# Decoder with a mixture of experts: a set's down weights queued ahead of the next set's gate weights

## What is computed

```python
for l in range(DEPTH):                      # DEPTH = 2
    h = rms_norm(x, norm1_g[l])
    proj = h @ w_in[l]                      # 1024 x 3072, then two kinds of attention
    ...
    x = x + jnp.concatenate([o_da, o_sb], axis=-1) @ w_out[l]
    h2 = rms_norm(x, norm2_g[l])
    x = x + hierarchical_moe(h2, ...)

# hierarchical_moe: best group of 4, then the two best of its 8 experts; combine holds their weights
hg = jnp.einsum('sd,edf->sef', hs, w_gate)  # 32 experts, 1024 x 256 each
hu = jnp.einsum('sd,edf->sef', hs, w_up)    # the same size
act = jax.nn.silu(hg) * hu * combine.astype(hs.dtype)[..., None]
return jnp.einsum('sef,efd->sd', act, w_down)   # 256 x 1024 each
```

## Time and profile before

| | us |
|---|---|
| median of 3 runs | 832.82 |
| lowest and highest | 831.23, 833.08 |
| the profiled execution's own time | 830.57 |
| its span, first to last instruction | 828.8 |
| PE busy in the span | 681.0 (82%) |
| DVE busy | 300.5 (36%) |
| ACT busy | 127.5 (15%) |
| DMA queue of SP, share of 16 engines | 72.3% |

### The profile page before, as it was taken

One profiled execution on the slowest core, in us unless ns is written; L12 is line 12 of the kernel. 1 busy time (PEld: TensorE's weight loads), 2 busy tenths in 40 slices (PEclk: granted clock), 3 DMA queues, 4 the chain that ended last, 5 costly groups with the idle time before them and its releaser, 6 DMA issues.

```text
span 828.8 us, 9937 instructions
## 1 busy us (share of the span) xinstructions
PE 681.0 (82%) x3684; PEld 335.2 (40%) x3685; DVE 300.5 (36%) x654; ACT 127.5 (15%) x318; POOL 9.0 (1%) x19
## 2 busy tenths in 40 slices
PE   7998999968865956878699989998788768658684
PEld 5445455643333312442144455646433224124321
DVE  0336622453423322413325364325243324224223
ACT  3115521200000000000031343211000000000000
POOL 0000000010000000000020000000000000000000
PEclk9999999999988878989899989998999889889997
DMA  8798038539999999975993240753299999999551
GB/s 291 238 400 314 1 123 334 202 47 418 421 422 423 421 422 423 421 294 226 387 344 145 102 152 1 270 243 147 95 418 421 422 422 421 422 422 421 236 202 51
DMA packets 49984, 240.03 MB, mean 290 GB/s; under 512 B 7648, under 2 KB 7936, under 8 KB 25376
## 3 DMA queue, kind: packets, MB, share of 16 engines
q1 hardware_dynamic: 49344, 238.61, 72.3%
q0 software_dynamic: 608, 0.99, 1.0%
HBM read 238.54 MB, written 1.05 MB: 289 GB/s over the span
## 4 chain that ended last, share of the span: by engine, by line
PE 54%; DMA 22%; issue 11%; DVE 5%; PEldq 2%; PEld 2%; ACT 1%; SPq 1%; DVEq 1%; ACTq 1%
PE bank L1020 19%; DMA wbuf<-in_w_down 18%; PE bank L1167 7%; PE bank L1117 7%; PE bank L1145 5%; PE bank L1184 5%; PE bank L1195 3%; DMA wbuf<-in_w_up 3%; PE bank L1077 1%; PEldq L1186 1%; PE bank L1064 1%; DMA wbuf<-in_w_in 1%; SPq L326 1%; PE bank L1097 1%; PE bank L1040 1%
## 5 line engine op out<-in xcount | busy, mean ns | idle before, releaser
L1020 PE MATMUL bank<-wbuf,hTbuf 128*128 128x512 f32 x384 | 170.3, 600 | 2.6 <-DMA wbuf<-in_w_in 2.1
L1184 PE MATMUL bank<-wbuf,qkT 128*32 128x512 f32 x512 | 80.6, 758 | 62.5 <-DMA wbuf<-in_w_down 56.0
L1167 PE MATMUL bank<-wbuf,qkT 128*32 128x512 f32 x1024 | 113.2, 594 | 2.0 <-DVE qkT L756 1.1
L1020 PEld LDWEIGHTS bank<-wbuf,hTbuf 128*128 128x128 f32 x384 | 72.7, 192 | 90.7 <-issue 88.3
L1145 PE MATMUL bank<-qkT,xn 128*128 128x128 f32 x512 | 68.6, 297 | 29.2 <-issue 29.2
L1145 PEld LDWEIGHTS bank<-qkT,xn 128*128 128x128 f32 x512 | 65.5, 211 | 42.2 <-issue 42.1
L783 DVE TENSOR_TENSOR x_sb<-x_sb,bank 128x512 f32<-128x512 f32 x72 | 46.3, 684 | 77.9 <-PE bank L1195 77.9
L1167 PEld LDWEIGHTS bank<-wbuf,qkT 128*32 128x32 f32 x1024 | 32.5, 110 | 79.4 <-issue 76.3
L1184 PEld LDWEIGHTS bank<-wbuf,qkT 128*32 128x32 f32 x512 | 16.3, 128 | 116.4 <-issue 58.5
L1117 PE MATMUL bank<-wbuf,hTbuf 128*128 128x512 f32 x128 | 56.0, 593 | 0.0
L776 DVE COPY qkT<-bank 128x512 f32<-128x512 f32 x16 | 11.1, 692 | 93.6 <-PEq L1186 93.6
(11 more groups left out here) (195 smaller groups left out, 592.8 us busy)
## 6 DMA issues: line engine op xcount, KB each, us to landing
wbuf<-in_w_gate SPq DMA_DIRECT2D x64, 1024.0 KB, 21.5
wbuf<-in_w_up SPq DMA_DIRECT2D x64, 1024.0 KB, 21.9
wbuf<-in_w_down SPq DMA_DIRECT2D x64, 1024.0 KB, 16.1
wbuf<-in_w_in SPq DMA_DIRECT2D x24, 1024.0 KB, 14.2
wbuf<-in_w_out SPq DMA_DIRECT2D x8, 1024.0 KB, 6.2
x_sb<-in_x SPq DMA_DIRECT2D x2, 512.0 KB, 4.5
out<-x_sb SPq DMA_DIRECT2D x1, 1024.0 KB, 4.0
cst<-in_const SPq DMA_DIRECT2D x1, 548.0 KB, 13.8
```

The costliest lines, as they stand in the source:

```text
L1020: last = MM(ps[PROJ_BANK[i][t]][:, :], hT[:, k, t * P:(t + 1) * P], block_rows(i, k), start=(k == 0), stop=(k == KC - 1))
L1167: MM(ps[bank][j * SLOTS:(j + 1) * SLOTS, :].rearrange("p (a f) -> p a f", a=2), src[:, k, j * SLOTS:(j + 1) * SLOTS], halves[:, gate:up + ...
L1184: MM(ps[banks[h]][j * SLOTS:(j + 1) * SLOTS, :], src[:, c, j * SLOTS:(j + 1) * SLOTS], at[j][:, c * D + h * HALF:c * D + (h + 1) * HALF], ...
```

## The change

In `load_further_sets` the wait for `dn_used` and the four down parts behind it are moved ahead of the four gate parts of the next set. Nothing else is changed: the same DMAs, the same slots, the same waits.

```diff
                     sp_.wait_ge(gu_used, l * SETS + g)
                     load_up(l, g, LANES - 1)
+                    sp_.wait_ge(dn_used, l * SETS + g)
+                    for j in range(LANES):
+                        load_down(l, g, j)
                     if g + 1 < SETS:
                         for j in range(LANES):
                             load_gate(l, g + 1, j)
-                    sp_.wait_ge(dn_used, l * SETS + g)
-                    for j in range(LANES):
-                        load_down(l, g, j)
```

## The result

The changed kernel takes 851.73 us as a median of 4 runs (850.85 to 852.89), the kernel before 832.95 of 4 (831.23 to 834.24). The ratio is 1.0228 with a 95% interval of 1.0204 to 1.0252, 18.8 us slower. The forecast was 851. The profiled execution took 850.98 us, with a span of 849.2 against 828.8.

The account below looks back on a forecast made before the run. The prediction took transfers to set the pace up to `gate_up` of set 6, then PE. Delays of 7.9 and 6.8 us plus 3.8 for the clock made 18.5 us, so 851 us as a median, range 845 to 855.

Parts of the forecast that it names:

- The step that no down part's early landing could help: At `gate_up` of set 6, PE follows the last up part; earlier down parts bring nothing beyond 0.2 to 0.4 us.
- The hole: At each layer's first wait in `load_further_sets`, held gate parts leave the queue empty: 7.9 and 6.8 us late.
- the restart: At set 1, the empty queue's first part lands 4.7 us after issue, then each further part after 2.49.
- The later sets: Behind set 1, `dn_used` comes 12.2 or 10 us before the queue's end, so the queue stays full.
- The clock: PE's rest moves ahead of `gate_up` of set 6, which runs at a lower clock: 1.9 us a layer, 3.8 in all.
- The stop of 2.25 us in the gather: Layer 0, before `dn_used` of set 0: PE's stop for issue might shrink by 0 to 2.25 us; taken as 0.
- The sum: Whole kernel: 7.9 + 6.8 + 3.8 = 18.5 us slower, giving a median of 851 us.
- The estimate at 2.93 us a part: At the skill page's 358 GB/s transfer rate, the two layers' shifts would be some 8.4 and 7.7 us.
- a hole in every set: Rival: `dn_used` comes after the queue's end in sets 2 to 6, 74 us more, 925 us; chance 0.04.
- a covered hole: Rival: queue still busy at the first wait, or PE slack at set 6, swallows the delay: 833 us; chance 0.04.
- the waits given back: Rival: PE's eight waits for down parts vanish, up to 56 us back, about 792 us; chance 0.03.
- part of the sum: Rival: the clock stays up and the 2.25 us stop shrinks, 12.4 us slower, 845 us; within the forecast case's 0.89.

Follow-up runs that it names:

- e3: Kernel before with the new order in the sets 2 to 4 alone: 835.18 us, ratio 1.0009 to the kernel before.
- e12: Kernel before, order of transfers kept, but at set 1 SP waits for `dn_used` ahead of the gate parts of set 2: 850.76 us, ratio 1.0203.
- e2: Kernel before with the new order in set 1 alone: 853.27 us, ratio 1.0208 to the kernel before.
- e5: Changed kernel with two of the four gate parts of set 2 ahead of the wait of set 1: 843.97 us, ratio 1.0120 to the kernel before.
- e6: Changed kernel where SP at set 1 also waits until `gate_up` of set 1 is done: 877.81 us, ratio 1.0552 to the kernel before.
- e1: Kernel before with the new order in the sets 2 to 6 alone, set 1 unchanged: 839.66 us, ratio 1.0084 to the kernel before.
- e4: Kernel before with the new order in set 5 alone: 837.07 us, ratio 1.0028 to the kernel before.
- e7: Changed kernel with 46 small unused matmuls in PE's rest ahead of the `gate_up` of set 6: 848.60 us, ratio 1.0186 to the kernel before.
- e10: Kernel before with 5 and 3 unused 512-column matmuls in PE's rests behind `gate_up` of set 6 and set 7: 821.43 us, ratio 0.9860.
- e8: Kernel before with 40 and 22 small unused matmuls in PE's rests behind `gate_up` of set 6 and set 7: 910.68 us, ratio 1.0919.
- e9: Changed kernel with 5 unused 512-column matmuls in PE's rest ahead of `gate_up` of set 6: 848.62 us, ratio 1.0191 to the kernel before.

## Why the prediction was right

**The place of the loss.** The step that no down part's early landing could help, since the queue's last up part of set 6 is what PE runs into, held: PE's waits for down parts went from 56.0 us to none and the kernel got slower. The order as such costs nothing that could be measured (e3, at most 2.8 us), and without any change of order the wait costs the same within the intervals (e12).

**The hole.** Predicted 7.9 and 6.8 us, measured 9.0 and 8.2 from set 0 to set 6. Here a term was too small, by 1.1 and 1.4 us: the restart. I took 4.7 us and then 2.49 a part, which puts the landing of the fourth down part some 10.8 us behind its issue; it took 12.4. The trace shows one step out of line in each layer, between the first and the second landing: 4.03 us (199.7 to 203.7) and 3.82 (620.9 to 624.7), instead of 2.49. In both a load of PE's instructions, 16 KB on the queue of instructions, begins close by (200.9 and 620.3). The kernel before has such a step too, 3.28 us (193.6 to 196.9) and 3.66 (609.6 to 613.3), with loads at 194.7 and 609.7. It is inside the landings that I compared with, so I had it on one side alone. That the load causes the step is not shown. For it speaks that the restarts of e2, e5 and e12 have both, a load and a step of 3.6 to 3.9 us, while in e6 (layer 0, restart at 208.14) and e1 (layer 1, at 629.26) no load begins between the first two landings or up to 2 us ahead of them, and these are 2.49 and 2.51 us apart. Against it speaks that the loads at 200.9 and 620.3 in the kernel before, beside a full queue, move no landing (2.47 and 2.49), and that e6 has a step of 3.09 us in layer 1 without a load near it.

**The size follows the wait.** 9.9 us less hole gave 8.8 us less time (e5, where the interval is 4.5 us to either side; the two stages have 8.2 less), and some 12 us more in each layer gave 24.7 us more by the medians (e6: 43.5 against 18.8), where the two stages account for 24.8.

**The later sets.** The margin of some 10 us held: the waits of the sets 2 to 6 end 8.9 to 12.2 us before the queue's last landing, the share of the DMA engines is 1.01 from 218 to 366 us, and the period 29.8 us. What the prediction doesn't say is that the hole at set 1 makes a part of this margin: without it the wait of set 2 comes too late in layer 1 (e1, e3).

**The clock.** Predicted 1.9 a layer, bounds 0 and 2.4. The `gate_up` of set 6 took 2.05 and 1.43 us more than 7.07, 3.5 instead of 3.8. In e1 and e4 it took up to 2.9 us more, beyond my upper bound: that bound was only the slowest cold `down` on record, and nothing showed that a `gate_up` can't lose more. That it is the clock is shown by the granted clock in the profile and by e7, where PE had no rest and the `gate_up` took 7.07. That it reaches the path behind set 6 is read from the stages, in the changed kernel (1.6 us more in each layer) and in e4; that it doesn't in the sets before, from the timeline of e3. The totals alone don't separate these 3.5 us: e2 and e12, with a warm `gate_up` of set 6, have intervals that hold both 15.3 and 18.8 us. The page "TensorE: Matmul & The Clock Gate" of the Trainium skill, Part 1, puts the ramp's penalty under 1% of a typical kernel span. The 3.5 us are 0.4%, but the tail's cold gathers and `down`s, which e10 shortened, are another 7.7 us (6.22 and 5.30 against 3.83, 6.09 and 5.66 against 3.95), so that all of it on the path is some 1.3%. A sum without the term would have been off by it.

**The stop of 2.25 us in the gather**: its change was left at 0. It became 2.02 us, and the wait for `dn_used` ended at 194.97 instead of 195.07: right.

**The sum.** The hole 2.5 us too small and the clock 0.3 too large would make 20.7 for the profiled pair, which shows 20.4; the medians show 18.8 against a forecast of 18.5. The two medians moved less than the two profiled executions, by an amount that lies within the spread of the runs, so the closeness to 0.3 us is partly luck.

**The estimate at 2.93 us a part.** Its shifts of 8.4 and 7.7 us don't follow from the prediction's own sum. From the up part of set 1 to the last up part of set 2 there are twelve steps before the change, and eleven behind the restart after it. A slower part therefore makes the shift smaller, by 0.44 us: 7.5 and 6.4. The forecast doesn't use it, and the window on the changed kernel shows 422 GB/s.

**The rivals.** None of the four came. The one of a hole in every set is refuted by the full windows, that of a covered hole by e2, that of the waits given back by the period of 29.8 us, and that of part of the sum by the cold `gate_up` and the stop, which stayed.

## What to carry to other kernels

In a queue whose issuer waits on semaphores itself, the order of two groups of transfers matters less than what stands behind the later wait: look where the queue is empty when the wait begins, since there each held transfer with a free place costs its own time. Behind a full queue the same wait is free as long as it ends early enough before the queue's last landing. Here the first landing from an empty queue takes 4.7 to 4.9 us and each further one 2.49, so by estimate the wait has to end some 2.3 us ahead. It ended 3.7 us ahead in e1, layer 0, which was enough; 2.0, 1.1 and 0.7 us ahead cost 0.8, 1.3 and 1.6 us (e3, e1). Removing a hole early in the queue uses up such margins behind it. An engine's longest waits name the place where it catches up with the queue, not what sets the pace; ask when the last part of each step lands. Rests that can't be removed should stand ahead of work that is off the path, or be filled with short work, in few and long instructions (e10 against e8).

## What was not expected of the hardware

- The length of PE's loop: 102 more matmul calls in its code (40 in the further round of either parity, and 22) went with a rise of the loads on the queue of instructions from 20 to 78 and of the time from 834 to 911 us (e8), while 8 wider calls in the same places did not (21 loads, e10), nor did 46 ahead of a `gate_up` (e7, 22 loads).
- Two to five us appear or vanish ahead of the gather behind the `gate_up` of set 0: 26.1 us from the first to the second `gate_up` of layer 1 before, 25.9 in the changed kernel, 21.3 in e7 and 21.2 in e10, whose added matmuls don't run in that set. Before, PE stands 4.29 us there and then gathers in 5.25 us; in e10 it stands 0.89 and takes 3.83. That the position of the code decides it is a guess; no run tests it.
- The granted clock fell to 0.50 behind a rest of only 2.9 us, and only once PE was at work again (e9: 1.00 in the rest, 0.50 from 350.50 to 353.40 us), while with no rest ahead it stayed up (e7).
